# Layer 1 of a two-layer trunk step: both score maps of a query tile in one step, cached keys in a step of their own

## The chip, the core and the metric

The kernel is one launch on one NeuronCore of a Trainium2 chip. The metric is the device time of the launch in microseconds, median of several runs; less is better. The core has TensorE (PE: matmuls and transposes, with weight loads as a second stream, PEld), VectorE (DVE), ScalarE (ACT), GpSimd (POOL) and SyncE (SP, which here only starts weight loads). Each engine runs its own queue in order; semaphores tie the queues together. Matmul results land in PSUM, eight banks of 128 partitions x 512 fp32.

## What is computed

A two-layer trunk over 512 latent tokens and 128 context tokens, 2048 wide. Layer 0 is a gated MLP beside grouped-query attention. Layer 1, which the change touches, is differential attention with 16 heads: each head has two maps with 64-wide queries and keys, and one 128-wide value.

```python
def diff_attend(q, k, v, lam):
    scale = C_QK_DIM ** -0.5

    def block(qb):
        s = jnp.einsum('bqhmd,bshmd->bhmqs', qb, k).astype(F32) * scale
        p = jax.nn.softmax(s, axis=-1)
        w = (p[:, :, 0] - lam * p[:, :, 1]).astype(v.dtype)
        return jnp.einsum('bhqs,bshe->bqhe', w, v)
...
out = (o.reshape(b_, t, C_V_WIDTH) * jax.nn.silu(g)) @ w_out
```

Latent tokens read the 512 latent keys and 128 cached context keys in one softmax, so a query tile of 128 latent tokens has 640 keys; the context tile has 128 keys.

## The kernel before

**Projection.** Weights stream in as chunks of 512 columns: 16 slices of 128 rows (kt) for each chunk, 5 token tiles for each slice. fp32 is split in two parts, `hi` and `lo`, and each product is three matmuls (hi·hi, hi·lo, lo·hi). ACT casts a slice to `w_hi` (L676), DVE subtracts to get `w_lo` (L1032), both two slices ahead of PE, in a ring of four. A slot is one token tile of one slice: three matmuls of 512 columns (L495). A chunk has 80 slots.

**Attention beside it.** The attention of layer 1 is cut in steps, listed in `ORDER1`, and the list `AT1` says behind which slot each step is issued. Heads 0 to 11 take 60 slots each, in three groups (a loop of three chunks and four heads); heads 12 to 15 take 80 slots each, with the numbers of `AT1` times 6/5 (a loop of one chunk and one head). All three engines walk the same list: PE puts a step behind its slot; ACT and DVE put it behind the split of the slice in which the slot lies (slots 5k to 5k+4), in order. So within one slice ACT does one split and then the steps due, and so does DVE.

**The steps.** T0 to T2 turn q and k (transposes into PSUM bank 5, `TURN`; ACT casts the hi part, L626; DVE subtracts the lo part, L907, which frees the bank). S is one map of one query tile: 64 rows of the array, two halves of 320 keys into banks 6 and 7, three matmuls each (L382); then DVE takes the row maximum (L914) and scales it (L917), and ACT takes the exponential with its row sum (L637, with a read of the accumulator behind it). Eight S are wide (four query tiles, two maps), two are 128 keys wide (context tile). Behind both maps of tile u DVE combines them into one weight tile (`combine(u)`: L926, L928, L931). T3 to T9 turn the weights (T3 to T5 tiles 0 and 1, T6 to T8 tiles 2 and 3, T9 the context tile; PE L373). P multiplies with v (L391), B turns the result back (L398).

**Who waits for whom.** All turns, products and back turns share bank 5. PE starts T4 only when DVE has finished the subtract of T3 (`t_free`). PE starts T3 when `combine(1)` is done (`w_ready`), T6 when `combine(3)` is. On ACT the step T3 begins with the casts of v (L652, L653), on DVE with the subtracts of v (L968, L970), which wait for those casts. PE starts a score step when ACT has read the score before it (`s_exp`). `norm_out` of the head before is spread over DVE's steps. GpSimd loads the next head's q, k and v and rotates q and k (L1351 to L1358).

The two lists before:

```python
ORDER1 = ["T", "T", "T", "S", "S", "S", "S", "T", "S", "T", "S", "T", "S", "P", "S", "B", "S", "T", "S",
          "T", "T", "P", "B", "T", "P", "B"]
AT1 = [0, 2, 4, 7, 10, 14, 18, 24, 26, 28, 31, 32, 35, 36, 40, 41, 44, 45, 48, 49, 51, 52, 54, 56, 58, 59]
```

## Time and profile before

| | |
|---|---|
| median of 3 runs | 2920.69 us (2916.67 to 2921.15) |
| profiled execution, first to last instruction | 2917.0 us |
| granted TensorE clock, mean | 0.970 of 2.4 GHz |
| TensorE busy | 2717.5 us (93%) |
| VectorE busy | 1565.7 us (54%) |
| ScalarE busy | 1017.8 us (35%) |
| layer 1's groups of heads 0 to 11 | about 1503 to 2278 us |
| layer 1's heads 12 to 15 | to about 2576 us, 76.8 us each |

Starts and durations are in microseconds from the first instruction. Matmuls are pipelined and their ends are modelled, so the distance between starts says what TensorE spends; a wait shown in brackets can understate what was lost. Each attention step can be priced by taking two projection matmuls around it and subtracting the usual distance.

### The profile page before, as it was taken

Reading aid. Unit: us, or ns where it says so; the run is one execution under the profiler, and the core shown is the slowest. Engines: PE = TensorE matmul, PEld = TensorE weight load, DVE = VectorE, ACT = ScalarE, POOL = GpSimd, SP = SyncE. Lnnn points to the kernel's source line nnn. Section 1 sums busy time; section 2 is a strip of 40 time slices with the busy share of each in tenths; the row PEclk is TensorE's granted clock in tenths of the full one; section 3 lists DMA queues with packets and bytes.
Section 4 is the critical chain, followed back from the end, with each engine's and each line's share of the span. In section 5 each row is a group of like instructions: output and inputs, shape, how many; then the busy total and the mean of one; then the engine's idle time right before and its main releaser. Section 6 shows DMA issues by size and latency. Waiting matters only on the chain.

```text
span 2917.0 us, 40231 instructions
## 1 busy us (share of the span) xinstructions
PE 2717.5 (93%) x12498; PEld 2106.4 (72%) x12498; DVE 1565.7 (54%) x3018; ACT 1017.8 (35%) x2023; POOL 417.3 (14%) x483
## 2 busy tenths in 40 slices
PE   6799999999999899979999999999999999979995
PEld 3488777777777677767877777777777777757774
DVE  5762455555656644446245556655655555555443
ACT  6632343442333334323233333333333333333331
POOL 0000121121122100000121112222211211010001
PEclk9899999999999999989999999999999999979998
DMA  8833444433445545543322222222222222365444
GB/s 322 334 115 112 148 147 141 136 114 129 154 162 171 201 172 181 181 152 119 108 97 82 89 84 78 91 89 88 76 98 75 94 95 88 102 207 191 159 140 176
DMA packets 164952, 400.77 MB, mean 137 GB/s; under 512 B 12936, under 2 KB 14608, under 8 KB 159568
## 3 DMA queue, kind: packets, MB, share of 16 engines
q1 hardware_dynamic: 131104, 249.14, 26.2%
...
## 4 chain that ended last, share of the span: by engine, by line
PE 74%; DVE 13%; issue 4%; DVEq 4%; ACT 3%; DMA 2%; SPq 0%; ACTq 0%; POOL 0%; POOLq 0%
PE ps L495 55%; PE ps L515 5%; PE ps L382 5%; PE ps L373 3%; DVE w_lo L1032 3%; PE ps L391 3%; DMA w_raw<-in_w_ada_dram 1%; DVE small L914 1%; ACT w_hi L676 1%; DVE work L931 1%; PE ps L474 1%; DVEq L1106 1%; DVE work L1126 1%; PE ps L525 1%; DVE small L835 1%
## 5 line engine op out<-in xcount | busy, mean ns | idle before, releaser
L495 PE MATMUL ps<-w_hi,hT_hi 128*128 128x512 f32 x2800 | 1155.9, 413 | 7.9 <-issue 7.9
L495 PE MATMUL ps<-w_hi,hT_lo 128*128 128x512 f32 x2800 | 1103.6, 394 | 0.0
L495 PE MATMUL ps<-w_lo,hT_hi 128*128 128x512 f32 x2800 | 1100.5, 393 | 0.0
L1032 DVE TENSOR_TENSOR w_lo<-w_raw,w_hi 128x512 fp32r<-128x512 f32 x944 | 641.4, 707 | 683.6 <-ACT w_hi L676 668.0
L676 ACT CAST w_hi<-w_raw 128x512 fp32r<-128x512 f32 x944 | 570.6, 620 | 503.3 <-PE ps L495 452.0
L495 PEld LDWEIGHTS ps<-w_hi,hT_hi 128*128 128x128 f32 x2800 | 531.6, 190 | 136.5 <-issue 42.7
L495 PEld LDWEIGHTS ps<-w_hi,hT_lo 128*128 128x128 f32 x2800 | 529.7, 189 | 117.8
L495 PEld LDWEIGHTS ps<-w_lo,hT_hi 128*128 128x128 f32 x2800 | 532.0, 190 | 89.5
L637 ACT ACTIVATE work<-ps,small 128x640 f32<-128x640 f32 (+1 forms) x192 | 139.1, 725 | 563.8 <-DVE small L917 563.7
L515 PE MATMUL ps<-w_hi,cst 128*128 128x512 f32 x384 | 193.9, 505 | 40.2 <-DVE w_lo L1032 30.4
L914 DVE TENSOR_REDUCE small<-ps 128x1 f32<-128x640 f32 (+1 forms) x200 | 143.7, 718 | 123.4 <-PE ps L382 116.2
L515 PEld LDWEIGHTS ps<-w_hi,cst 128*128 128x128 f32 x384 | 78.7, 205 | 139.5 <-DVE w_lo L1032 126.6
L515 PE MATMUL ps<-w_lo,cst 128*128 128x512 f32 x384 | 162.1, 422 | 0.0
L907 DVE TENSOR_TENSOR wT_lo<-ps,wT_hi 128x512 fp32r<-128x512 f32 (+2 forms) x168 | 93.6, 557 | 114.8 <-ACT wT_hi L626 113.2
L626 ACT CAST wT_hi<-ps 128x512 fp32r<-128x512 f32 (+2 forms) x168 | 80.5, 479 | 212.4 <-PE ps L373 211.8
L373 PE MATMUL ps<-consts,work 128*128 128x128 f32 x744 | 122.8, 282 | 28.7 <-DVE work L931 17.4
L373 PEld LDWEIGHTS ps<-consts,work 128*128 128x128 f32 x744 | 89.5, 142 | 80.8 <-DVE work L931 24.0
L382 PE MATMUL ps<-kT_hi,qT_hi 64*128 64x320 f32 (+1 forms) x360 | 123.6, 343 | 5.1 <-ACT work L637 4.9
L382 PEld LDWEIGHTS ps<-kT_hi,qT_hi 64*128 64x128 f32 (+1 forms) x360 | 66.3, 184 | 64.3 <-issue 47.6
L382 PE MATMUL ps<-kT_lo,qT_hi 64*128 64x320 f32 (+1 forms) x360 | 108.7, 302 | 0.0
L382 PE MATMUL ps<-kT_hi,qT_lo 64*128 64x320 f32 (+1 forms) x360 | 108.5, 301 | 0.0
L474 PE MATMUL ps<-consts,work 128*128 128x128 f32 x320 | 55.8, 314 | 53.4 <-DVEq L1106 34.9
...
## 6 DMA issues: line engine op xcount, KB each, us to landing
...
```

The costliest lines, as they stand in the source:

```text
L373: last = nc.tensor.transpose(ps[:, TURN, n * P:(n + 1) * P], src, ident)
L382: last = nc.tensor.matmul(ps[:, SC + b, 0:w], qT[x][r0:r0 + L.dk, q0:q0 + P], kT[y][r0:r0 + L.dk, k0:k0 + w], start=(i == 0), stop=(i == 2))
L391: last = nc.tensor.matmul(ps[:, TURN, 0:width], vv[x][:, vt, :], wT[y][:, k, 0:width], start=(k == 0 and i == 0), stop=(k == len(tiles) - ...
L474: last = nc.tensor.transpose(ps[:, TURN + t // TS, t % TS * P:(t % TS + 1) * P], slot(F, kt // 4)[:, t, kt % 4 * P:(kt % 4 + 1) * P], ident)
L495: last = nc.tensor.matmul(ps[:, t, :], x[:, kt, t * P:(t + 1) * P], w[:, kt % RING, :], start=(kt == 0 and i == 0), stop=(kt == KT - 1 and ...
L515: last = nc.tensor.matmul(ps[:, MOD, :], cst[:, kt * 4:kt * 4 + P], w[:, kt % RING, :], start=(kt == 0 and i == 0), stop=(kt == KT - 1 and ...
L626: last = nc.scalar.copy(dst, ps[:, TURN, c0:c1])
L637: nc.scalar.activation(dst if src.ndim == 2 else dst.rearrange("p (b w) -> p b w", b=2), src, ACT.Exp, bias=small[:, 20 + m:21 + m], scale ...
L676: nc.scalar.copy(w_hi[:, kt % RING, :], w_raw[:, i % RAW, kt % 2, :]).then_inc(w_hi_ready, 1)
L907: last_op = nc.vector.tensor_tensor(lo, ps[:, TURN, c0:c1], hi.bitcast(F32), ALU.subtract)
L914: nc.vector.tensor_reduce(small[:, 22 + m:23 + m], src, AX_X if src.ndim == 2 else mybir.AxisListType.XY, ALU.max)
L1032: nc.vector.tensor_tensor(w_lo[:, kt % RING, :], w_raw[:, i % RAW, kt % 2, :], w_hi[:, kt % RING, :].bitcast(F32), ALU.subtract).then_inc( ...
```

## The change

For layer 1 the step S becomes one step for both maps of a query tile over the 512 latent keys: map 0 on array rows 0 to 63 into bank 6, map 1 on rows 64 to 127 into bank 7, matmuls in pairs. A new step C computes, once for each head, the scores of all four query tiles against the 128 cached keys, both maps, in both banks; ACT copies them to SBUF (`ctx_scores`, in `ws_t`). X is the context tile, both maps. K is a step of DVE alone: the first takes the maxima of the cached-key scores, the others are `combine(0)` to `combine(4)`, which was inside the S steps before. ACT's exponentials for a tile are now four: two of 512 from PSUM, which release the banks (`s_exp`), and two of 128 from SBUF, which release `combine` (`s_full`). DVE takes both maxima in one instruction and adds the two row sums. `rope_a`, `gq` and `gk` share one buffer, GpSimd rotates in place, layer 1's gate bias lies in `ws_t` and is loaded some instructions later, and `norm_out` advances at every step.

```diff
-ORDER1 = ["T", "T", "T", "S", "S", "S", "S", "T", "S", "T", "S", "T", "S", "P", "S", "B", "S", "T", "S",
-          "T", "T", "P", "B", "T", "P", "B"]
+ORDER1 = ["T", "T", "T", "C", "K", "S", "K", "S", "K", "S", "T", "T", "T", "K", "S", "P", "B", "K", "X", "T", "T", "T",
+          "K", "P", "B", "T", "P", "B"]
...
-AT1 = [0, 2, 4, 7, 10, 14, 18, 24, 26, 28, 31, 32, 35, 36, 40, 41, 44, 45, 48, 49, 51, 52, 54, 56, 58, 59]
+AT1 = [0, 2, 4, 8, 11, 12, 19, 20, 27, 28, 30, 32, 34, 36, 37, 39, 42, 43, 44, 46, 47, 49,
+       50, 51, 53, 54, 57, 59]
...
-        gq = sb("gq", [P, P])
-        gk = sb("gk", [P, P])
+        scr = sb("scr", [P, 6 * P])
+        rope_a = scr[:, 0:4 * P]
+        gq = scr[:, 4 * P:5 * P]
+        gk = scr[:, 5 * P:6 * P]
...
-        gate_bias = rope_a[:, :]
         ws_t = sb("ws_t", [P, 1024])
+        gate_bias = [rope_a, ws_t[:, 0:NC]]
+        ctx_scores = ws_t
...
+        ctx_sums = small[:, 78:86]
+        ctx_max = small[:, 86:94].rearrange("p (m u) -> p m u", m=2)
...
+        def diff_pe(pe, h):
...
+            def both_maps(out, q0, k0, width):
+
+                for i, (x, y) in enumerate(((0, 0), (0, 1), (1, 0))):
+                    for m in range(2):
+                        r = slice(64 * m, 64 * m + 64)
+                        last = nc.tensor.matmul(ps[:, SC + m, out:out + width], qT[x][r, q0:q0 + P],
+                                                kT[y][r, k0:k0 + width], start=(i == 0), stop=(i == 2))
+                return last
+
...
+                elif kind == "C":
+                    pe.wait_ge(s.t_free, h * NF + 4)
+                    scores_free(0)
+                    for t in range(TS):
+                        last = both_maps(t * P, t * P, TS * P, P)
+                    last.then_inc(s.s_ready, 1)
+                elif kind == "S":
+                    scores_free(1 + u)
+                    both_maps(0, u * P, 0, NC).then_inc(s.s_ready, 1)
+                    u += 1
+                elif kind == "X":
+                    scores_free(5)
+                    both_maps(0, TS * P, NTOK, P).then_inc(s.s_ready, 1)
...
+        def diff_act(act, h):
...
+            def exponent(dst, src, n, total):
+                m, u = n % 2, n // 2
+                return nc.scalar.activation(dst, src, ACT.Exp, bias=small[:, 20 + 2 * (u % 2) + m:21 + 2 * (u % 2) + m],
+                                            scale=L1.scale, accum_out=total[:, n:n + 1])
...
+                elif kind == "C":
+                    act.wait_ge(s.s_ready, h * 6 + 1)
+                    nc.scalar.copy(ctx_scores[:, :], ps[:, SC:SC + 2, :].rearrange("p a b -> p (a b)")).then_inc(s.s_exp, 1)
+                elif kind in ("S", "X"):
+                    act.drain()
+                    act.wait_ge(s.w_ready, h * 5 + (u + 1))
+                    act.wait_ge(s.s_max, h * 5 + (u + 1))
+                    dst = weights[:, 0:2, 0:NC] if kind == "S" else weights[:, 0:2, 0:P]
+                    width = NC if kind == "S" else P
+                    for m in range(2):
+                        last = exponent(dst[:, m, :], ps[:, SC + m, 0:width], 2 * u + m, sums)
+                    last.then_inc(s.s_exp, 1)
+                    if kind == "S":
+                        for m in range(2):
+                            at = (m * TS + u) * P
+                            last = exponent(weights[:, m, NC:NTOK], ctx_scores[:, at:at + P], 2 * u + m, ctx_sums)
+                        last.then_inc(s.s_full, 1)
+                    u += 1
+                elif kind == "P":
...
+        def diff_dve(dve, h, before):
...
+            def context_max():
+
+                dve.drain()
+                dve.wait_ge(s.s_exp, h * 6 + 2)
+                nc.vector.tensor_reduce(small[:, 86:94], ctx_scores.rearrange("p (x k) -> p x k", k=P), AX_X, ALU.max)
+                dve.drain()
+                nc.vector.tensor_scalar(small[:, 86:94], small[:, 86:94], -L1.scale, None, ALU.mult)
+
+            def scores(u):
+
+                bias = small[:, 20 + 2 * (u % 2):22 + 2 * (u % 2)]
+                dve.drain()
+                dve.wait_ge(s.s_ready, h * 6 + (u + 2))
+                nc.vector.tensor_reduce(small[:, 24:26], ps[:, SC:SC + 2, 0:NC if u < TS else P], AX_X, ALU.max)
+                dve.drain()
+                if u < TS:
+                    nc.vector.scalar_tensor_tensor(bias, small[:, 24:26], -L1.scale, ctx_max[:, :, u],
+                                                   ALU.mult, ALU.min).then_inc(s.s_max, 1)
+                else:
+                    nc.vector.tensor_scalar(bias, small[:, 24:26], -L1.scale, None, ALU.mult).then_inc(s.s_max, 1)
+
+            def combine(u):
+
+                width = 640 if u < TS else P
+                dst = weights[:, 2 + u % 2, :] if u < TS else wts_p[:, :]
+                n = slice(2 * u, 2 * u + 2)
+                dve.drain()
+                if u < TS:
+                    dve.wait_ge(s.s_full, h * 4 + (u + 1))
+                    nc.vector.tensor_tensor(sums[:, n], sums[:, n], ctx_sums[:, n], ALU.add)
+                    dve.drain()
+                else:
+                    dve.wait_ge(s.s_exp, h * 6 + 7)
+                nc.vector.reciprocal(inv_sums[:, n], sums[:, n])
+                dve.drain()
+                nc.vector.scalar_tensor_tensor(small[:, 26:27], sums[:, 2 * u:2 * u + 1], small[:, 12:13],
+                                               inv_sums[:, 2 * u + 1:2 * u + 2], ALU.mult, ALU.mult)
+                dve.drain()
+                nc.vector.scalar_tensor_tensor(dst, weights[:, 1, 0:width], small[:, 26:27], weights[:, 0, 0:width],
+                                               ALU.mult, ALU.add).then_inc(s.w_ready, 1)
...
+                elif kind in ("S", "X"):
+                    scores(n)
+                    n += 1
+                elif kind == "K":
+                    if k == 0:
+                        context_max()
+                    else:
+                        combine(k - 1)
+                    k += 1
...
-                    nc.gpsimd.tensor_tensor(rope_a[:, :], flat, rope_c[:, :], ALU.mult)
                     z4 = flat.rearrange(halves, s=2, j=half)
                     b4 = rope_b[:, :].rearrange(halves, s=2, j=half)
                     s4 = rope_s[:, :].rearrange(halves, s=2, j=half)
                     for k in range(2):
                         nc.gpsimd.tensor_tensor(b4[:, :, k, :], z4[:, :, 1 - k, :], s4[:, :, k, :], ALU.mult)
                     pool.drain()
-                    nc.gpsimd.tensor_tensor(flat, rope_a[:, :], rope_b[:, :], ALU.add)
+                    nc.gpsimd.tensor_tensor(flat, flat, rope_c[:, :], ALU.mult)
+                    pool.drain()
+                    nc.gpsimd.tensor_tensor(flat, flat, rope_b[:, :], ALU.add)
...
-            wait(gb_free, 4)
-            load_bias(1, 0)
             wait(S[1].v_split, 16)
             load_y(1, 0)
             store_head(L1, 14)
             free_head(L1, 14)
             wait(S[1].t_ready, 160)
+            wait(gb_free, 4)
+            load_bias(1, 0)
```

The order in which the instructions stand changes on all three engines. Three places show it, all in a head of the groups, from the score step of the last tile ahead of the first weight transpose to that transpose.

ACT before: exponential (L637), split (L676), v casts, T3's cast, split, exponential, T4's cast (L626).

```order
L637 ACTIVATE work,ssq<-ps,small 128x640
...
L676 CAST w_hi<-w_raw 128x512
...
L652 CAST v_hi<-work 128x640
L653 CAST v_hi<-work 128x128
L626 CAST wT_hi<-ps 128x512
...
L676 CAST w_hi<-w_raw 128x512
...
L637 ACTIVATE work,ssq<-ps,small 128x640
L626 CAST wT_hi<-ps 128x512
```

ACT after: L769 is the exponential, L819 the split, L783 and L784 the v casts, L764 the casts of T3 and T4.

```order
L769 ACTIVATE work,ssq<-ps,small 128x512 x2
L769 ACTIVATE work,small<-ws_t,small 128x128 x2
...
L819 CAST w_hi<-w_raw 128x512
...
L783 CAST v_hi<-work 128x640
L784 CAST v_hi<-work 128x128
...
L764 CAST wT_hi<-ps 128x512
...
L764 CAST wT_hi<-ps 128x512
```

Before, the exponential ahead of the v casts is that of tile 1's second map; now it is tile 2's, four instructions, and its slot (28) lies two slots ahead of T3 (30).

DVE before: maximum, split, `combine(1)` (L926 to L931), v subtracts, T3's subtract.

```order
L914 TENSOR_REDUCE small<-ps 128x1
L917 TENSOR_SCALAR small<-small 128x1
...
L1032 TENSOR_TENSOR w_lo<-w_raw,w_hi 128x512
...
L926 RECIPROCAL ssq<-ssq 128x2
L928 SCALAR_TENSOR_TENSOR small<-ssq,small 128x1
L931 SCALAR_TENSOR_TENSOR work<-work,small 128x640
...
L968 TENSOR_TENSOR v_lo<-work,v_hi 128x640
L970 TENSOR_TENSOR v_lo<-work,v_hi 128x128
L907 TENSOR_TENSOR wT_lo<-ps,wT_hi 128x512
```

DVE after: `combine(1)` (L1083 to L1092), tile 2's maximum (L1067, L1070), split (L1275), v subtracts, T3's subtract (L1051).

```order
L1083 TENSOR_TENSOR ssq<-ssq,small 128x2
L1087 RECIPROCAL ssq<-ssq 128x2
L1089 SCALAR_TENSOR_TENSOR small<-ssq,small 128x1
L1092 SCALAR_TENSOR_TENSOR work<-work,small 128x640
...
L1067 TENSOR_REDUCE small<-ps 128x2
L1070 SCALAR_TENSOR_TENSOR small<-small 128x2
...
L1275 TENSOR_TENSOR w_lo<-w_raw,w_hi 128x512
...
L1120 TENSOR_TENSOR v_lo<-work,v_hi 128x640
L1122 TENSOR_TENSOR v_lo<-work,v_hi 128x128
...
L1051 TENSOR_TENSOR wT_lo<-ps,wT_hi 128x512
```

A whole maximum of tile 2 now stands between `combine(1)` and the subtract that frees the bank for T4.

PE before, from a wide S (slot 26) to the T behind it (28): six matmuls, all on one half of the rows.

```order
L382 MATMUL ps<-kT_hi,qT_hi 128x320
L382 MATMUL ps<-kT_lo,qT_hi 128x320
L382 MATMUL ps<-kT_hi,qT_lo 128x320
L382 MATMUL ps<-kT_hi,qT_hi 128x320
L382 MATMUL ps<-kT_lo,qT_hi 128x320
L382 MATMUL ps<-kT_hi,qT_lo 128x320
...
L373 MATMUL ps<-consts,work 128x128 x4
```

PE after, from S of tile 2 (slot 28) over T3 (30) to T4 (32); L580 is the projection.

```order
L488 MATMUL ps<-kT_hi,qT_hi 128x512 x2
L488 MATMUL ps<-kT_lo,qT_hi 128x512 x2
L488 MATMUL ps<-kT_hi,qT_lo 128x512 x2
L580 MATMUL ps<-w_hi,hT_hi 128x512
...
L480 MATMUL ps<-consts,work 128x128 x4
...
L480 MATMUL ps<-consts,work 128x128 x4
```

There were four slots between T3 and T4; there are two.

## Rows read from the trace of the kernel before

**Rows 1.** The page: busy time, share of the span and instructions of each engine.
```profile
PE 2717.5 (93%) x12498; PEld 2106.4 (72%) x12498; DVE 1565.7 (54%) x3018; ACT 1017.8 (35%) x2023; POOL 417.3 (14%) x483
```

**Rows 2.** Windows: stretch, length; PE, PEld, DVE, ACT, POOL busy (count); clock, DMA, GB/s.
```profile
1780.00:2040.00 260.00, 248.09 (x1207) 190.71 (x1205) 151.53 (x319) 90.40 (x206) 55.95 (x59) 0.99 0.26 85
```

**Rows 3.** Timeline, a wide score step: start, duration, engine, line, tiles, forms.
```profile
2393.60 0.39 PE L495 MATMUL ps<-w_lo,hT_hi 128*128 128x512 f32 x1
...
2393.83 0.39 PE L495 MATMUL ps<-w_hi,hT_lo 128*128 128x512 f32 x1
...
2394.83 0.30 PE L382 MATMUL ps<-kT_lo,qT_hi 64*128 64x320 f32 x1
...
2394.98 0.31 PE L382 MATMUL ps<-kT_hi,qT_lo 64*128 64x320 f32 x1
...
2395.56 0.40 PE L495 MATMUL ps<-w_lo,hT_hi 128*128 128x512 f32 x1
```

**Rows 4.** Timeline, 1800 to 1803: a narrow score step, then a weight transpose.
```profile
1800.70 0.39 PE L495 MATMUL ps<-w_hi,hT_lo 128*128 128x512 f32 x1
...
1801.84 0.40 PE L495 MATMUL ps<-w_lo,hT_hi 128*128 128x512 f32 x1
...
1802.31 0.60 PE L373 MATMUL ps<-consts,work 128*128 128x128 f32 x4
...
1802.98 0.39 PE L495 MATMUL ps<-w_lo,hT_hi 128*128 128x512 f32 x1
```

**Rows 5.** Waits of TensorE, 1503 to 2576: total, times, longest.
```profile
PE ps L373 <- DVE work L931: 17.4, 13, 2.1
...
PE ps L382 <- ACT work L637: 4.9, 8, 1.3
PE ps L391 <- DVE wT_lo L907: 3.6, 16, 0.2
```

**Rows 6.** Groups by form, 1520 to 2278: busy, mean ns of one, idle before.
```profile
L914 DVE TENSOR_REDUCE small<-ps 128x1 f32<-128x640 f32 x91 | 75.1, 825 | 35.7 <-PE ps L382 30.8 <-issue 1.8
...
L914 DVE TENSOR_REDUCE small<-ps 128x1 f32<-128x128 f32 x24 | 7.0, 292 | 13.2 <-PE ps L382 12.9
...
L637 ACT ACTIVATE work<-ps,small 128x640 f32<-128x640 f32 x91 | 72.5, 796 | 269.4 <-DVE small L917 269.4
...
L637 ACT ACTIVATE work<-ps,small 128x128 f32<-128x128 f32 x24 | 8.8, 368 | 54.8 <-DVE small L917 54.8
```

**Rows 7.** Timeline of one head: exponential, split, v, combination, first weight transpose.
```profile
1832.21 0.79 ACT L637 ACTIVATE work<-ps,small 128x640 f32<-128x640 f32 x1 [5.23 <-DVE small L917]
...
1833.00 0.61 ACT L676 CAST w_hi<-w_raw 128x512 fp32r<-128x512 f32 x1
...
1837.65 0.72 ACT L652 CAST v_hi<-work 128x640 fp32r<-128x640 f32 x1
...
1838.28 0.29 ACT L653 CAST v_hi<-work 128x128 fp32r<-128x128 f32 x1
1838.64 0.17 DVE L926 RECIPROCAL ssq<-ssq 128x2 f32<-128x2 f32 x1 [0.16 <-issue]
...
1839.97 0.82 DVE L968 TENSOR_TENSOR v_lo<-work,v_hi 128x640 fp32r<-128x640 f32 x1
1840.11 0.66 PE L373 MATMUL ps<-consts,work 128*128 128x128 f32 x4 [1.47 <-DVE work L931]
...
1841.42 0.69 DVE L907 TENSOR_TENSOR wT_lo<-ps,wT_hi 128x512 fp32r<-128x512 f32 x1 [0.43 <-ACT wT_hi L626]
```

**Rows 8.** Timeline: a combination that stands beside GpSimd's rotation.
```profile
1828.99 1.98 DVE L931 SCALAR_TENSOR_TENSOR work<-work,small 128x640 f32<-128x640 f32 x1
```

**Rows 9.** A window behind a loop boundary (columns as in Rows 2), and TensorE's timeline there.
```profile
1748.00:1750.00 2.00, 2.00 (x6) 1.61 (x7) 0.69 (x1) 0.62 (x1) 0.00 (x0) 0.50 0.90 364
...
1747.99 0.79 PE L495 MATMUL ps<-w_hi,hT_hi 128*128 128x512 f32 x1 [3.54 <-issue]
...
1751.47 0.40 PE L495 MATMUL ps<-w_hi,hT_hi 128*128 128x512 f32 x1
```

142 lines of the change are left out of this document (130 added, 12 removed).

## The prediction

> **What bounds the kernel now.** The page comes first: TensorE is busy 93% of the span, no other engine over 54% [rows 1]. Then the windows, because an average over stages hides the stage in question: in one group of four heads TensorE is busy 248 of 260 us, VectorE 152 and ScalarE 90 [rows 2]. So layer 1's attention is bound by TensorE, and what TensorE spends on it counts in full. But the other two engines have slack only on average. The timeline shows how a head really runs: one score, its maximum, its exponential, and the next thing TensorE wants often depends on the end of that chain. The table of waits says how much of that is visible already: 17.4 us for combined weights, 4.9 for an exponential, 3.6 for a subtract ahead of a product [rows 5]. Starts lie a little further apart than these idle times say, so I take 30 us in all for the waits that this schedule now has and that the new one replaces.
>
> **What the change saves on TensorE.** Two projection matmuls start 0.23 us apart. From the last one ahead of a wide score step to the second behind it are 1.73 us; less two distances of 0.23, a wide score step costs 1.27 us [rows 3]. Its six matmuls of 320 columns start 0.15 apart (0.87), so 0.40 is the step's fixed part. A narrow one costs 1.14 - 0.46 = 0.68 [rows 4]. A head has eight wide and two narrow: 11.5 us. After the change, if the two matmuls of a pair run at once, S costs 0.40 + 3 x 0.23 = 1.09, four of them 4.4. C has 12 pairs of 128 columns. Transposes of that width start 0.11 us apart (four take 0.60, one about 0.27) [rows 4], so C is 0.35 + 12 x 0.11 = 1.7 if the weight loads of a pair overlap too and 0.35 + 24 x 0.11 = 3.0 if they do not; I take 2.2, nearer to overlap, since the matmuls are assumed to. X lies between 0.7 and 1.0, I take 0.8. Sum 7.4, saved 4.1 us a head, **66 us for 16 heads** (bounds 50 and 79). If pairs do not overlap at all, S is 0.40 + 6 x 0.23 = 1.78, the sum 11.1, and only some 5 us are saved.
>
> No row of this trace has two row halves at work together. The Trainium skill (TensorEngine Tiling (Array Packing), Key Properties) says that different tiles can execute loads and matmuls in parallel, which is the first case; whoever leaves the page out is left with the two bounds, 66 and 5.
>
> **What the change adds: the wait between T3 and T4.** This is the term that decides, and it does not lie on TensorE. T4 needs the bank that T3 filled, and the bank is free when DVE has done T3's subtract. On ACT the four exponentials of tile 2 stand ahead of T3's cast, since S of tile 2 is now in slot 28 and T3 in slot 30. I follow the chain from the end of `combine(1)`, which TensorE needs for T3 as well:
> - DVE, maximum over 1024 elements: 0.825 us at 640 and 0.292 at 128 give 1.04 ns an element, so 1.22 us [rows 6]; with the drains around it and the small instruction, 1.6 until ACT starts.
> - ACT, two exponentials of 512: 0.796 at 640 and 0.368 at 128 [rows 6] give 0.69; with the accumulator read and the overlap of neighbours (1832.21 to 1833.00 is 0.79 for 640 wide [rows 7]) 0.68 each, the narrow ones 0.36 each. Together 2.1.
> - ACT, the split of the next slice, which starts 0.5 ahead of what follows it, then the casts of v, 0.63 + 0.29 [rows 7]. Together 1.4.
> - DVE, v subtracts: 0.82 with the next one starting a little early, the second taken as long as the cast of its size, 0.29; with a drain 1.1. T3's subtract 0.69 [rows 7], and 0.1 for signals.
>
> The sum is 7.0 us. In that time TensorE has T3 (0.45: 1802.98 - 1801.84 less three distances of 0.23 [rows 4]) and two slots (1.4). So if TensorE is at T3 when `combine(1)` ends, it stands for 5.2 us at T4.
>
> Is it there at that time? One tile's round from maximum to maximum is: 3.7 to the end of the exponentials as above, split on ACT 0.6, split on DVE 0.7, `combine` 1.6 (1838.64 to 1840.11 with its drain [rows 7]) and 0.24 for the added sum: 6.9 us. TensorE spends 8 x 0.69 + 1.09 = 6.6 on the way from S to S. The round is the longer one, so faster matmuls only lead to earlier waits. Undisturbed, from S of tile 0 to T4 the chain takes 1.0 + 2 x 6.9 + 7.0 = 21.8 us and TensorE's own work 17.5: **4.3 us of waiting**. But GpSimd rotates the next head's q and k in this stretch, and beside it a combination took 1.98 us instead of 0.9 [rows 8], and in one head of four an evacuation of five copies stands in ACT's queue. I add 2.2, so 6.5 in all, of which some 5 at T4 and the rest at T3 and at S of tile 2. Twelve heads: 78 us. In heads 12 to 15 the slots are a fifth further apart; from S of tile 2 TensorE has 5.0 us of its own, the chain 7.9: 2.9 each, 12 us. **Sum 90** (bounds 64 without the disturbances, 108 with them doubled).
>
> **The smaller terms.** T7 follows T6 by one slot. T6, its cast and its subtract take 0.60 + 0.59 + 0.69 and gaps, 2.0 us; TensorE has 0.45 + 0.69 of its own: 0.9 at least, and ACT may come late from X's exponentials; I take 1.5, **24 us** (14 to 37). T9 behind its back turn and the group boundaries: **7 us**. The clock: after a wait of 3.54 us at a loop boundary the granted clock was 0.50 in the next two microseconds, that is 1.2 instead of 2.4 GHz, and from 1747.99 to 1751.47 TensorE did six projection matmuls and one turn of four, 6 x 0.23 + 0.45 = 1.8 us at full clock, in 3.5 [rows 9]. So such a wait costs 1.6 us more, for twelve heads **19 us** (0 if the wait at T4 stays shorter than that one). DVE's work for C, the rotation in place (same instruction count, one drain more) and the later gate bias (one issue, behind the last turn of head 15) hide beside the projection; if the bias comes late it costs under a microsecond, once.
>
> **The sum.** 90 + 24 + 7 + 19 = 140 us more, 66 + 30 = 96 us less: +44 on the profiled execution of 2917.0, which gives 2961. The runs' median lies 3.7 above that span: **2965 us**.
>
> The Trainium skill (TensorEngine Tiling (Array Packing), PSUM Bottleneck) warns that row tiling speeds up TensorE and not the evacuation of PSUM, which may then be the bound. That is this sum's direction; the page gives no figure for it, and nothing above is taken from it.
>
> **Rivals.**
> 1. *The pairs do not overlap.* Then 5 instead of 66 are saved (+61). Each S is 0.7 longer, so TensorE arrives about 2 us later at T4 in the groups and 0.7 in the last heads, which takes back 27. Result 2999. For it: all matmuls of the trace run one behind the other. Against: they all share rows or banks with their neighbours.
> 2. *Not slower: the ACT and DVE chain ahead of T4 is shorter than its parts.* Place: the subtract of T3. The gain of 96 stands against 24 + 7, and against 19 only if the clock falls; without that it pays as long as the heads wait less than 65 / 16 = 4.1 us each, where I have 5.6. The undisturbed 4.3 and 2.9 are close to that point. If the chain halves this to 2 to 2.5 a head with a full clock, 90 + 19 become 36: 2892. For it: the margin is small, and two of the three instructions I price by their size have no row of their own. Against: the queue order is fixed, and six instructions stand in it.
> 3. *Gain and waits cancel*: chain undisturbed, short T7, clock kept: 64 + 17 + 7 - 96 = -8, about 2915.
> 4. *Worse than the sum*: the clock stays at its lower level through more of each head, since T7, T3 and S wait as well; doubled clock term and upper bounds, 3030.
>
> **How the numbers follow.** Forecast 0.54, pairs serial 0.17, faster chain 0.14, cancel 0.08, worse 0.07. The forecast's own range is 2925 to 3005: all lower bounds but that of the clock at one end, all upper ones at the other. To hold 8 in 10 the range takes in the serial case and the upper part of "worse", and below the cancelling one: 2908 to 3025. A measurement of this kernel tells about 0.2% (6 us) from no change. Faster: the faster chain and half of the cancelling case, 0.18. Within 0.2%: part of the other half and the forecast's lowest end, 0.06. Slower: 0.76.
>
> **What would show it.** Pairs: the two matmuls of a pair start within some 10 ns and a wide step costs 1.1 us, not 1.8. The chain: in the table of waits a new line of some 60 us, TensorE's transpose waiting for DVE's `wT_lo`, longest about 5 us, 12 to 16 large ones, and ACT's v cast right behind four exponentials. The clock: windows behind T4 at 0.5. VectorE busy share must stay near 54%. The forecast is wrong if the transposes wait under 2 us at T4, or if groups of heads take less than 260 us; it is right for a wrong reason if the extra time lies outside 1503 to 2576.

## The result: slower by 3.9%, more than forecast

| kernel | median, us (lowest to highest) | ratio to the kernel before (95%) |
|---|---|---|
| before | 2920.92 (2916.67 to 2924.34) | 1 |
| changed | 3033.51 (3029.88 to 3037.02) | 1.0385 (1.0368 to 1.0401) |

The forecast was 2965, range 2908 to 3025. The direction was right and the main mechanism was there. The loss, +113 us, is more than twice the +44 of the sum, and the time lies 8 us above the range.

From the page of the changed kernel, the line of busy shares and the first line of its chain. TensorE is at 89% instead of 93% [rows 1], with the same number of instructions; the chain that ended last goes through TensorE for only 61% of the span.

```profile
PE 2706.4 (89%) x12498; PEld 2088.7 (69%) x12498; DVE 1595.2 (53%) x2954; ACT 1060.7 (35%) x2295; POOL 416.0 (14%) x483
...
PE 61%; DVE 19%; ACT 6%; DVEq 5%; issue 5%; DMA 2%; ACTq 2%; SPq 0%; POOL 0%; POOLq 0%
```

Everything ahead of 1503 us takes as long as before. Layer 1's stretch of projection and attention took 1503 to 2576 before and takes 1503 to 2692 now: 116 us, the whole difference. The window over it (columns as in [rows 2]) shows TensorE busy 1024 of 1189 us, at a granted clock of 0.93:

```profile
1503.00:2692.00 1189.00, 1024.13 (x5021) 780.87 (x5020) 651.11 (x1247) 415.62 (x1113) 209.44 (x222) 0.93 0.25 79
```

**The pairs work.** TensorE's timeline at a wide score step. `x2` means that both maps' matmuls are in the row. They start together, and the third pair starts 0.23 us after the second. Priced like the step of [rows 3], from the projection matmul at 1939.59 to the second one behind the step less two distances of 0.23, the step costs 1.09 us, as forecast.

```profile
1939.59 0.39 PE L580 MATMUL ps<-w_hi,hT_lo 128*128 128x512 f32 x1
1939.91 0.50 PE L488 MATMUL ps<-kT_hi,qT_hi 64*128 64x512 f32 x2
1940.24 0.39 PE L488 MATMUL ps<-kT_lo,qT_hi 64*128 64x512 f32 x2
1940.47 0.39 PE L488 MATMUL ps<-kT_hi,qT_lo 64*128 64x512 f32 x2
1940.80 0.50 PE L580 MATMUL ps<-w_hi,hT_hi 128*128 128x512 f32 x1
```

C costs 1.68 us and X 0.69, so the scores of a head fall from 11.5 to 6.73 us. Over 16 heads TensorE saves 77 us.

**The waits.** TensorE's waits from 1500 us on (total, times, longest), against those of [rows 5]. L480 is a transpose step, L488 a score step, L769 the exponential, L1051 the subtract of a turn.

```profile
PE ps L480 <- DVE wT_lo L1051: 102.5, 32, 5.5
PE ps L488 <- ACT work L769: 37.3, 13, 4.5
PE ps L480 <- DVE work L1092: 7.9, 11, 1.3
```

The first line stands for two waits a head, 32 in all: T4's, up to 5.5 us, and T7's, 1.5 to 2.

**The chain of T4, one head.** Rows of all engines from the end of `combine(1)` to T4 (L1092 combination, L1067 maximum, L819 the split of the next weight slice, L783 and L784 the casts of v, L764 the cast of T3):

```profile
1887.49 0.88 DVE L1092 SCALAR_TENSOR_TENSOR work<-work,small 128x640 f32<-128x640 f32 x1
1888.43 0.66 PE L480 MATMUL ps<-consts,work 128*128 128x128 f32 x4 [0.76 <-DVE work L1092]
1888.54 1.23 DVE L1067 TENSOR_REDUCE small<-ps 128x2 f32<-128x1024 f32 x1 [0.16 <-issue]
...
1890.38 0.69 ACT L769 ACTIVATE work<-ps,small 128x512 f32<-128x512 f32 x1 [4.55 <-DVE small L1070]
...
1892.49 0.61 ACT L819 CAST w_hi<-w_raw 128x512 fp32r<-128x512 f32 x1
1893.00 0.73 ACT L783 CAST v_hi<-work 128x640 fp32r<-128x640 f32 x1
...
1893.83 0.58 ACT L764 CAST wT_hi<-ps 128x512 fp32r<-128x512 f32 x1
1893.96 0.82 DVE L1120 TENSOR_TENSOR v_lo<-work,v_hi 128x640 fp32r<-128x640 f32 x1
...
1895.18 0.69 DVE L1051 TENSOR_TENSOR wT_lo<-ps,wT_hi 128x512 fp32r<-128x512 f32 x1 [0.20 <-issue]
...
1895.93 1.12 PE L480 MATMUL ps<-consts,work 128*128 128x128 f32 x4 [5.45 <-DVE wT_lo L1051]
```

From T3 to T4 are 7.50 us, where the prediction had 7.0 from the end of `combine(1)`. Between them stand the instructions that it named, in its order. The maximum is 1.23 for 1.22 expected, an exponential 0.69 for 0.69.

**The clock behind it.** A window that begins with this T4 has a granted clock of 0.56, and the matmuls of the projection in it stand 0.43 us apart instead of 0.23:

```profile
1896.00:1902.00 6.00, 6.00 (x19) 4.90 (x20) 1.96 (x4) 1.48 (x3) 2.07 (x3) 0.56 0.36 122
```

```profile
1897.27 0.63 PE L580 MATMUL ps<-w_lo,hT_hi 128*128 128x512 f32 x1
1897.70 0.63 PE L580 MATMUL ps<-w_hi,hT_lo 128*128 128x512 f32 x1
```

### The profile page after: what moved, and what is told of

It is laid out like the page before. It is cut to its first block, busy times and chain, and to the rows that moved or that the text cites. A ratio compares the mean times of both kernels' runs of the same rounds, so it can differ in the third digit from the quotient of the medians.

```text
span 3032.0 us, 40647 instructions
## 1 busy us (share of the span) xinstructions
PE 2706.4 (89%) x12498; PEld 2088.7 (69%) x12498; DVE 1595.2 (53%) x2954; ACT 1060.7 (35%) x2295; POOL 416.0 (14%) x483
## 4 chain that ended last, share of the span: by engine, by line
PE 61%; DVE 19%; ACT 6%; DVEq 5%; issue 5%; DMA 2%; ACTq 2%; SPq 0%; POOL 0%; POOLq 0%
PE ps L580 46%; PE ps L600 5%; DVE w_lo L1275 3%; ACT work L769 3%; DVE small L1067 3%; PE ps L480 2%; ACT w_hi L819 2%; DVE work L1092 2%; PE ps L535 2%; DMA w_raw<-in_w_ada_dram 1%; ACTq L791 1%; PE ps L559 1%; DVEq L1080 1%; PE ps L488 1%; PE ps L379 1%
## 5 line engine op out<-in xcount | busy, mean ns | idle before, releaser
L580 PE MATMUL ps<-w_hi,hT_hi 128*128 128x512 f32 x2800 | 1171.1, 418 | 13.6 <-issue 7.3
L580 PE MATMUL ps<-w_hi,hT_lo 128*128 128x512 f32 x2800 | 1118.7, 400 | 0.0
L580 PE MATMUL ps<-w_lo,hT_hi 128*128 128x512 f32 x2800 | 1116.7, 399 | 0.0
L1275 DVE TENSOR_TENSOR w_lo<-w_raw,w_hi 128x512 fp32r<-128x512 f32 x944 | 648.2, 714 | 786.4 <-ACT w_hi L819 770.8
L819 ACT CAST w_hi<-w_raw 128x512 fp32r<-128x512 f32 x944 | 569.1, 620 | 502.8 <-PE ps L580 452.2
L580 PEld LDWEIGHTS ps<-w_hi,hT_hi 128*128 128x128 f32 x2800 | 543.3, 194 | 149.2 <-issue 41.3
L580 PEld LDWEIGHTS ps<-w_hi,hT_lo 128*128 128x128 f32 x2800 | 540.2, 193 | 121.5
L580 PEld LDWEIGHTS ps<-w_lo,hT_hi 128*128 128x128 f32 x2800 | 543.5, 194 | 94.0
L769 ACT ACTIVATE work<-ps,small 128x512 f32<-128x512 f32 (+1 forms) x160 | 98.3, 619 | 407.2 <-DVE small L1070 336.4
L480 PE MATMUL ps<-consts,work 128*128 128x128 f32 x496 | 96.2, 317 | 114.5 <-DVE wT_lo L1051 102.5
L480 PEld LDWEIGHTS ps<-consts,work 128*128 128x128 f32 x496 | 65.1, 160 | 164.9 <-DVE wT_lo L1051 122.9
L1051 DVE TENSOR_TENSOR wT_lo<-ps,wT_hi 128x512 fp32r<-128x512 f32 (+2 forms) x112 | 62.4, 557 | 111.3 <-ACT wT_hi L764 108.2
L1598 POOL TENSOR_TENSOR work<-work,rope_s 128x256 f32<-128x256 f32 x96 | 80.0, 851 | 247.7 <-DVEq L1014 162.3
L764 ACT CAST wT_hi<-ps 128x512 fp32r<-128x512 f32 (+2 forms) x112 | 53.7, 479 | 160.6 <-PE ps L480 160.6
L559 PE MATMUL ps<-consts,work 128*128 128x128 f32 x320 | 55.6, 313 | 51.5 <-DVEq L1349 32.9
L1067 DVE TENSOR_REDUCE small<-ps 128x2 f32<-128x1024 f32 (+1 forms) x80 | 85.2, 1065 | 15.9 <-issue 9.1
L1570 POOL DMA_DIRECT2D work<-z x48 | 41.6, 869 | 376.3 <-PE ps L480 279.4
L488 PE MATMUL ps<-kT_hi,qT_hi 64*128 64x128 f32 (+1 forms) x288 | 57.0, 392 | 37.3 <-ACT work L769 37.3
```

Source lines behind the costliest of these rows:

```text
L480: last = nc.tensor.transpose(ps[:, TURN, n * P:(n + 1) * P], src, ident)
L488: last = nc.tensor.matmul(ps[:, SC + m, out:out + width], qT[x][r, q0:q0 + P], kT[y][r, k0:k0 + width], start=(i == 0), stop=(i == 2))
L559: last = nc.tensor.transpose(ps[:, TURN + t // TS, t % TS * P:(t % TS + 1) * P], slot(F, kt // 4)[:, t, kt % 4 * P:(kt % 4 + 1) * P], ident)
L580: last = nc.tensor.matmul(ps[:, t, :], x[:, kt, t * P:(t + 1) * P], w[:, kt % RING, :], start=(kt == 0 and i == 0), stop=(kt == KT - 1 and ...
L769: return nc.scalar.activation(dst, src, ACT.Exp, bias=small[:, 20 + 2 * (u % 2) + m:21 + 2 * (u % 2) + m], scale=L1.scale, accum_out=total ...
L819: nc.scalar.copy(w_hi[:, kt % RING, :], w_raw[:, i % RAW, kt % 2, :]).then_inc(w_hi_ready, 1)
```

## Where the 116 us went

The timeline gives the start of each step and of each projection matmul in the stretch. From the distance over a step I take what the step costs undisturbed.

| what | forecast | found in starts |
|---|---|---|
| T4 over its own 0.45 us, 16 heads | } | 91 |
| S steps over 1.09 us | } 90 | 45 |
| T3 over 0.45 us | } | 12 |
| T7 | } 31, with T9 and the group boundaries | 29 |
| chunk ends and loop boundaries | } | about 6 |
| projection matmuls 0.40 us or more apart (half clock) | 19 | 42 |
| score steps themselves | -66 | -77 |
| waits of the schedule before | -30 | -30 (as forecast, not counted anew) |
| sum | +44 | +118, against 116 |

In the stretch 186 distances between projection matmuls lie between 0.40 and 0.65 us and cost 43.6 us over 0.23; before there were 8, 2.0 us. That is the clock's line of the table.

The two ends agree better than the lines do. Counted by starts, the kernel before waited 20 us at T3, 6 at its score steps and 8 at its second product, 34 and not 30. About 7 us of slow distances right behind a step stand in the step's line and in the clock's as well. And T5 and T8, each the last part of a group of turns, have no line: they cost 12 us over their undisturbed time now and 3 before.

The block of waits was forecast with 90 and is 148: T4 alone takes what was meant for all three. Most of the rest stands in front of S. The rows of DVE and GpSimd behind a maximum show why. L1602 and L1600 are GpSimd's rotation of the next head's q and k; L980, L1083 and L1089 work on 1 to 5 columns; L1033 is a piece of the normalisation of the head before:

```profile
1943.87 1.28 POOL L1602 TENSOR_TENSOR work<-work 128x512 f32<-128x512 f32 x1
1944.08 1.10 DVE L980 SCALAR_TENSOR_TENSOR small<-small 128x5 f32<-128x5 f32 x1
...
1947.46 1.56 POOL L1600 TENSOR_TENSOR work<-work,rope_c 128x512 f32<-128x512 f32 x1
1948.04 1.00 DVE L1083 TENSOR_TENSOR ssq<-ssq,small 128x2 f32<-128x2 f32 x1 [0.17 <-issue]
...
1949.16 1.28 POOL L1602 TENSOR_TENSOR work<-work 128x512 f32<-128x512 f32 x1
1949.36 1.10 DVE L1089 SCALAR_TENSOR_TENSOR small<-ssq,small 128x1 f32<-128x1 f32 x1
...
1951.52 0.82 DVE L1033 TENSOR_TENSOR work<-work,gsub 128x640 f32<-128x640 f32 x1
```

Away from the rotation L980 takes 0.17, L1083 0.16 and L1089 0.22 (at 1941.79, 1886.72 and 1887.20). Here each ends within 0.03 us of the GpSimd instruction beside it: 1945.18 and 1945.15, 1949.04 and 1949.02, 1950.46 and 1950.44. They are held until GpSimd is through. The Trainium skill (SBUF — State Buffer, Who interferes with whom) gives that rule: a VectorE instruction with two inputs in SBUF contends with a GpSimd instruction that reads SBUF, and the ports that they share are an exclusive lock. The trace agrees by these three ends, and by the instructions with at most one SBUF input, whose means do not move with the rotation (below).

So the first round, from the maximum of tile 0 to that of tile 1, is here 11.1 us (1942.27 to 1953.39), not 6.9. S of tile 2, at 1956.45, waited 3.36 us for the exponentials at the end of that round. It is so in every head of the groups that was measured (heads 1 to 11): the first round takes 11.1 to 11.4 us and the second 7.0. In the head above neither the rotation nor a piece of the normalisation stands in the second.

## Experiments

The theory: TensorE waits at S and T4 for a chain of VectorE and ScalarE, and the order of steps and their slots put that chain there, not the pairs. Rivals: the slots alone are at fault; the pairs are worth nothing; the half clock is the loss; the rotation or the normalisation costs every kernel the same. The kernel before, timed anew beside each group of experiments, took 2917.7 to 2919.3 us.

### The order and the slots

**S2 behind the turns.** S of tile 2 is put behind T5, and the slots are set so that TensorE finds each step ready.

```
-ORDER1 = [T, T, T, C, K, S, K, S, K, S, T, T, T, K, S, P, B, K, X, T, T, T, K, P, B, T, P, B]
-AT1 = [0, 2, 4, 8, 11, 12, 19, 20, 27, 28, 30, 32, 34, 36, 37, 39, 42, 43, 44, 46, 47, 49, 50, 51, 53, 54, 57, 59]
+ORDER1 = [T, T, T, C, K, S, K, S, K, T, T, T, S, K, P, S, B, K, T, X, T, T, K, P, B, T, P, B]
+AT1 = [0, 2, 4, 7, 8, 10, 10, 21, 21, 33, 36, 38, 38, 38, 41, 41, 44, 44, 51, 51, 53, 55, 55, 56, 57, 58, 59, 59]
```

> The changed kernel with its step functions untouched and only the two lists altered: the score step of tile 2 stands behind T5 instead of ahead of T3, and the slots leave room (T3 33, T4 36, T5 38, S of tiles 2 and 3 in 38 and 41, X 51). Theory (the order in ScalarE's and VectorE's queues makes the waits, the steps themselves are sound): T4 no longer stands behind four exponentials, its wait falls from about 5.7 us a head to under 1, the waits of the wide scores from 45 us in all to under 10, and the 77 us that the paired matmuls save on TensorE become visible: 2850 us, 2830 to 2890, and so faster than the kernel before. Rival (the paired form as such is too dear for the other two engines: more exponentials, wider maxima): the waits only move to other steps, 2990 to 3050.

Measured 2874.17 us (2867.20 to 2879.92), ratio 0.9853 (0.9832 to 0.9873): 159 us less than the changed kernel and faster than the kernel before, with the same arithmetic. It came out 24 us above the 2850 expected, within its range, and the waits (L478 is the transpose, L578 the projection here) say where the rest is: not at T4 any more, but at the projection, for a split.

```profile
PE ps L578 <- DVE w_lo L1273: 19.9, 14, 3.0
PE ps L478 <- DVE wT_lo L1049: 8.7, 24, 0.5
```

**The order alone.** The same table, with S of tile 2 back ahead of T3.

```
-ORDER1 = [T, T, T, C, K, S, K, S, K, T, T, T, S, K, P, S, ...]
-AT1 = [0, 2, 4, 7, 8, 10, 10, 21, 21, 33, 36, 38, 38, 38, 41, 41, ...]
+ORDER1 = [T, T, T, C, K, S, K, S, K, S, T, T, T, K, P, S, ...]
+AT1 = [0, 2, 4, 7, 8, 10, 10, 21, 21, 30, 33, 36, 38, 38, 41, 41, ...]
```

> The version with S2 behind the turns (2874.2 us), with its slots, but S2 put back ahead of T3 (slot 30) as in the changed kernel. It tells the order from the slots. Theory: S2's maxima and exponentials stand on VectorE and ScalarE ahead of the combination, copies and splits that T4 waits for, some 3 us on each; with 3 slots between T3 and T4, T4 waits again: 2950 (2925 to 2975). Rival, only the slots matter: 2885 or less.

Measured 2945.61 us (2940.45 to 2950.01), ratio 1.0090 (1.0062 to 1.0117), as expected. The wait of the turns is back, and only that one; the waits of S for an exponential are 0.9 us in all:

```profile
PE ps L478 <- DVE wT_lo L1049: 59.3, 28, 4.6
```

So one step moved past three, with its slot, is worth 71 us (2945.6 against 2874.2), 4.5 a head. Of these 51 stand in the turns' wait (59.3 against 8.7) and 20 in distances at half clock (24.5 against 4.9). The maximum, exponentials and combination of a tile whose scores no one needs yet stood ahead of work that T4 needed.

**Room alone.** The changed kernel's order, with four more slots between T3 and T4.

```
-AT1 = [..., 27, 28, 30, 32, 34, 36, 37, 39, ...]
+AT1 = [..., 27, 28, 30, 36, 38, 38, 38, 39, ...]
```

> The changed kernel with its order of steps, and only the slots of T4 (32 to 36), T5 (34 to 38), K3 and S3 (to 38) changed: four more slots of projection, some 2.8 us, lie between T3 and T4. Theory, the wait of T4 is the time from T3 through combination, copies, splits and rounding less what TensorE has to do meanwhile: the wait falls from 5.5 to about 2.7 us, 45 us over 16 heads, of which a part comes back in front of S3, P0 and T7, and the half clock behind it goes, up to 20 us: 2980 (2965 to 3000). Rival, a round of engines without end of which T4 is only one place: the time lost moves to other steps and the total stays within 10 us of 3033.

Measured 3004.12 us (3001.43 to 3004.98), ratio 1.0297 (1.0280 to 1.0315): 29 us less, where 54 were expected. The transposes' waits fell by 37 us as the theory has it, to at most 2.7 us. But 16.5 us of waits for the first product's copy (L806) came up, as P and B keep their old slots, and S still waits. The rival, that the total stays within 10 us of 3033, is out too:

```profile
PE ps L478 <- DVE wT_lo L1049: 65.6, 32, 2.7
PE ps L486 <- ACT work L767: 34.7, 12, 4.1
PE ps L540 <- ACT oT L806: 16.5, 16, 1.8
```

The four tables make a ladder: 3033.5 as it is, 3004.1 with room at T4, 2945.6 with the table of "S2 behind the turns" but S of tile 2 ahead of T3, 2874.2 with S of tile 2 moved as well. The last step, S of tile 2 alone, is worth 71 us. The 88 us ahead of it come from the slots, and from two changes of order that go with them: the first P stands ahead of S of tile 3, and T6 ahead of X. No run parts these from the slots. So the rival "only the slots" is out, and the place of S of tile 2 isn't the whole either.

### What stretches the chain

**No rotation.** Layer 1's rotary embedding is left out, GpSimd's work of that stretch.

```
-                for z in (q_in, k_in):
+                for z in (q_in, k_in) if L.n == 0 else ():
```

> The changed kernel without the rotary rotation of q and k in layer 1 (GpSimd's four instructions per tensor are left out there; layer 0 keeps it). Theory: the extra 45 us of waits at the wide scores come from VectorE's small instructions that take 1.0 to 1.3 us beside GpSimd's rotation instead of 0.2; without it these waits fall to about 10 us, T4's wait stays at 5 us a head: 2985 us, 2965 to 3005. Rival (the waits at the scores come from the round's own length and from the instructions of norm_out): under 15 us are gained, 3018 or more.

Measured 2985.78 us (2985.29 to 2986.35), ratio 1.0228 (1.0209 to 1.0246): 48 us less than the changed kernel, as expected. The wait at T4 did not move:

```profile
PE ps L480 <- DVE wT_lo L1051: 104.7, 32, 5.5
```

L488's wait for an exponential is 4.8 us in all here, where it was 37.3. The distances at half clock fell as well, from 43.6 to 31.5 us. The first round takes 8.8 us instead of some 11.2, and the second 7.0 as before. By form, from 1503 to 2576 us, the small instruction L1083 has a mean of 161 ns here and 347 in the changed kernel, L980 165 and 280, the split L1275 691 and 770. The maximum L1067, which reads PSUM, has 1224 and 1225, and the turn's subtract L1051, with one input in PSUM, 689 and 690.

**The same in the kernel before.**

```
-                for z in (q_in, k_in):
+                for z in (q_in, k_in) if L.n == 0 else ():
```

> The kernel before with layer 1's rotary embedding left out (its GpSimd work; the output is another). On the changed kernel this gave 48 us. Theory: there VectorE's short instructions, stretched beside GpSimd, stand in a chain that TensorE waits for; before they do not, so little changes: 2914 (2908 to 2919) against 2918. Rival, the rotation costs every kernel the same through VectorE: 2870 to 2890.

Measured 2905.2 us (2899.92 to 2907.89), ratio 0.9956 (0.9942 to 0.9969): 13 us, somewhat more than the 4 expected, a quarter of the 48. VectorE's instructions were stretched before as well (the split of weights had a mean of 715 ns, and 688 without rotation), but TensorE hardly stood behind them: its wait for combined weights fell from 17.4 to 9.8 us and that for an exponential from 4.9 to nothing. The price of a disturbance depends on who waits.

**Normalisation off K and X.** The pieces of the normalisation of the head before are no longer advanced at the steps K and X, so they don't stand between a maximum and the combination.

```
-                next(before, None)
+                if kind not in ("K", "X"):
+                    next(before, None)
```

> The changed kernel with norm_out of the head before not advancing at the steps K and X, so that none of its pieces stands between the maxima of the cached keys and the maximum of tile 0, nor between combine(0) and the maximum of tile 1 (0.8 us each). They run behind the scores instead, beside ScalarE's exponentials. Theory: the round of tiles 0 to 2 gets 1 to 1.6 us shorter in the twelve heads of the groups: 3017 us, 3008 to 3025. Rival (those pieces are hidden, the round is held by ScalarE and the rotation): 3033, within 5.

Measured 3004.59 us (3002.64 to 3009.77), ratio 1.0296 (1.0274 to 1.0318): 29 us less, where 16 were expected. The first round takes 9.7 to 9.8 us in heads 1 to 10. S's wait falls to 11.4 us and the distances at half clock to 29.9, while T3's wait grows:

```profile
PE ps L480 <- DVE wT_lo L1051: 108.3, 32, 5.5
PE ps L480 <- DVE work L1092: 19.1, 18, 1.3
PE ps L488 <- ACT work L769: 11.4, 9, 2.6
```

**Both: S2 behind the turns, normalisation off K and X.** The two edits above, together.

> The version with S2 behind the turns, with the normalisation of the head before not advanced at the steps K and X. Theory: on the changed kernel this was worth 29 us because VectorE's chain set the length; here it does not, so little is left: 2868 (2860 to 2876) against 2874.2. Rival, VectorE's order still sets it: 2850 or less.

Measured 2847.01 us (2846.34 to 2849.68), ratio 0.9761 (0.9745 to 0.9777). This is the fastest: 71 us under the kernel before, 186 under the changed one. My expectation was wrong, and its rival right: VectorE's order still cost 27 us. I had looked at T4 and S, where little was left to gain. DVE's rows of the kernel without this edit show what was missed: a piece of the normalisation (L1031) beside the rotation takes 1.73 us instead of 0.82, the two splits behind it come late, and the projection waits 1.03 us for them.

```profile
1876.37 1.73 DVE L1031 TENSOR_TENSOR work<-work,gsub 128x640 f32<-128x640 f32 x1
1878.29 2.10 DVE L1273 TENSOR_TENSOR w_lo<-w_raw,w_hi 128x512 fp32r<-128x512 f32 x2 [0.19 <-issue]
...
1879.84 0.50 PE L578 MATMUL ps<-w_hi,hT_hi 128*128 128x512 f32 x1 [1.03 <-DVE w_lo L1273]
```

With the edit the projection's wait for splits in the stretch is 1.4 us in all, down from 19.9, which is 18.5 of the 27, and TensorE is busy 970 of its 1001 us:

```profile
1503.00:2504.00 1001.00, 969.60 (x5013) 743.25 (x5012) 637.60 (x1242) 416.13 (x1109) 208.20 (x222) 0.99 0.29 93
```

### What the pairs are worth

**Maps in turn (loops exchanged).**

```
-                for i, (x, y) in enumerate(((0, 0), (0, 1), (1, 0))):
-                    for m in range(2):
+                for m in range(2):
+                    for i, (x, y) in enumerate(((0, 0), (0, 1), (1, 0))):
```

> The changed kernel with only the pairing undone: in each score step the three matmuls of map 0 come first, then the three of map 1, so neighbours share the same half of the rows. Theory (VectorE and ScalarE's chain is the bound in each head): a wide step costs 1.8 instead of 1.09 us and C 3.0 instead of 1.68, together some 4.4 us a head or 71 us in all, but 60% of it is taken back by shorter waits at T4, T3 and the scores: 3062 us, 3050 to 3080. Rival (TensorE's own time still counts in full): 3033 + 71 = 3104.

Measured 3034.16 us (3029.05 to 3037.60), ratio 1.0398 (1.0378 to 1.0418), 0.7 us from the changed kernel: neither the 3062 of the theory nor the rival's 3104. The order of TensorE's instructions did change. In the built program map 0's three matmuls now stand ahead of map 1's three. The timeline still shows pairs:

```profile
1935.34 0.51 PE L488 MATMUL ps<-kT_hi,qT_hi 64*128 64x512 f32 x2
1935.67 0.40 PE L488 MATMUL ps<-kT_lo,qT_hi 64*128 64x512 f32 x2
```

A trace of the new order, and not a repeat of the old one, can be told by a small thing: read one by one, the two matmuls of a pair start 10 ns apart (median of 63 wide steps), and 3 ns in the changed kernel. So the edit did not undo the overlap, and its time says nothing of what the overlap is worth.

**Maps apart.** The same order, with a wait between the two triples that is always satisfied.

```
+                for m in range(2):
+                    if m == 1:
+                        pe.wait_ge(setup_in, 16 * N_SETUP)
+                    for i, (x, y) in enumerate(((0, 0), (0, 1), (1, 0))):
```

> The changed kernel, but the three matmuls of map 0 stand ahead of the three of map 1 in every scores step, with a wait that is always satisfied between them, so that the two halves of the rows no longer work on neighbouring matmuls (but for one at the joint). All other engines get the same work in the same order. Theory, the maxima, exponentials and splits from one step to T4 set the length of a head: the matmuls that are no longer paired lengthen TensorE's work by some 0.45 us a scores step and about 3 us a head, 45 us in all (from 0.23 us for a matmul of 512 columns), and part of that goes into waits that get shorter: 3055 (3045 to 3070) against 3033.5. Rival, TensorE's own work sets the length: all of it counts, 3079 or more. Rival, pairing was worth nothing: 3033.

> The version with S2 behind the turns (2874.2 us), with the maps apart in the same way. Here TensorE waits little, so the same 3 us a head should count in full: 2919 (2905 to 2935), which would say that the two halves of the rows are worth about 45 us once nothing else holds the engine. If other engines set the length here too, less than 20 us.

Measured 3033.30 us (3030.52 to 3038.03) and, for the version with S2 behind the turns, 2875.70 (2871.94 to 2885.36; ratio 0.9861): the times of 3033.5 and 2874.2 again, so the rival "pairing was worth nothing" seems right. The timeline says otherwise. Although map 0's three matmuls come ahead of map 1's, the trace has them side by side again, and the step still takes 1.09:

```profile
1881.86 0.50 PE L490 MATMUL ps<-kT_hi,qT_hi 64*128 64x512 f32 x2
1882.19 0.40 PE L490 MATMUL ps<-kT_lo,qT_hi 64*128 64x512 f32 x2
1882.42 0.41 PE L490 MATMUL ps<-kT_hi,qT_lo 64*128 64x512 f32 x2
```

The two halves of the rows had three matmuls each and worked them off at the same time. Map 1's first weight load, which carries the wait and stands in the program behind map 0's three matmuls, starts at 1881.86, 10 ns after map 0's first load and 0.33 us ahead of map 0's second matmul. Over the wide steps of both kernels the two matmuls of a pair start 10 ns apart in the median. The expectation was wrong in its premise, that only neighbours can overlap. The edit had not undone the cause.

**Map 1 waits for map 0.** A real dependency, on the fastest version.

```
+                for m in range(2):
+                    if m == 1:
+                        half[0] += 1
+                        last.then_inc(s.half, 1)
+                        pe.wait_ge(s.half, h * 9 + half[0])
```

> The version with S2 behind the turns and the normalisation off K and X (2847.0 us), but in every scores step the three matmuls of map 1 wait for the end of map 0's three, so that the two halves of the rows cannot work at once. Written order alone did not part them: with map 0's matmuls written ahead, the trace still shows both maps' rows at the same starts. Theory: side by side they save TensorE 0.23 us a matmul of 512 columns, and here TensorE sets the length: a wide step goes from 1.09 to 1.8 to 2.0 us (three more matmuls and the end of the third to wait for), C from 1.7 to some 3.8, X by 0.5, about 6 us a head and 96 us in all: 2943 (2915 to 2960), that is, no faster than the kernel before. Rival, other engines set the length and absorb it: below 2885.

Measured 2939.16 us (2935.38 to 2945.92), ratio 1.0081 (1.0054 to 1.0109), as expected, 92 us more than with pairs. Now the rows are single, and the second triple starts 0.45 us after the start of the first triple's last matmul:

```profile
1893.15 0.49 PE L493 MATMUL ps<-kT_hi,qT_hi 64*128 64x512 f32 x1
1893.49 0.39 PE L493 MATMUL ps<-kT_lo,qT_hi 64*128 64x512 f32 x1
1893.72 0.39 PE L493 MATMUL ps<-kT_hi,qT_lo 64*128 64x512 f32 x1
1894.17 0.50 PE L493 MATMUL ps<-kT_hi,qT_hi 64*128 64x512 f32 x1
```

In C the end of one quarter's map 1 and the start of the next quarter's map 0 have no wait between them, and there the triples run side by side again, out of the order in which they are written:

```profile
1886.65 0.27 PE L493 MATMUL ps<-kT_hi,qT_lo 64*128 64x128 f32 x1
1886.98 0.33 PE L493 MATMUL ps<-kT_hi,qT_hi 64*128 64x128 f32 x2
```

A wide step costs 2.10 instead of 1.09, C 3.17 instead of 1.68, X 0.61 more: 6.1 us a head, 98 over 16, of which 92 arrive in the time. Some 0.32 of each wide step's 1.01 is the wait for the end, which a kernel without pairs wouldn't have; without it 0.69, three matmuls of 0.23. The distances at half clock grew too, from 2.6 to 11.1 us, mostly behind C. So the 92 us are more than the pairs alone are worth. An estimate for those: 0.69 for each wide step, 12 x 0.11 for C and 3 x 0.11 for X are 4.4 us a head, 70 us in all. On a schedule that leaves TensorE the bound, lost time on TensorE counts nearly in full, so the pairs pay. Whether they pay on the changed kernel too, where TensorE waits, wasn't run.

### The clock

**The wait filled.** The changed kernel, with 14 more matmuls a head ahead of T4; their result is not used.

```
+                        if r == 4:
+                            scores_free(4)
+                            for _ in range(14):
+                                nc.tensor.matmul(ps[:, SC, 0:NC], qT[0][:, 0:P], kT[0][:, 0:NC], start=True, stop=True)
```

> The changed kernel with 14 matmuls more per head (512 columns, into the scores bank of map 0 once S2's exponentials have read it; S3 overwrites what they write), put ahead of T4, in the time that TensorE waits there: about 3.2 of the 5.5 us. Their result is not used, and nothing else changes. Theory, the half clock that follows each of these waits costs time of its own: after the wait at 1895.93 us a row of projections stands 0.43 us apart where it is 0.23 otherwise, 12 rows, 2.4 us a head, 38 us over 16 heads. With the wait filled the clock stays full and T4 starts as before, so the kernel gets faster although it does more: 2997 (2990 to 3010) against 3033.5. Rival, the half clock costs nothing of its own, as the engines behind it set the pace there too: 3030 to 3040. Rival, the matmuls delay T4: above 3040.

Measured 3018.41 us (3014.48 to 3020.70), ratio 1.0346 (1.0322 to 1.0369): 15 us less than the changed kernel, between the theory's 36 and the rival's nothing. The kernel does more and is faster, and the distances at half clock fell by 18 us, so the half clock has a price of its own. In the head from above T4 now waits 0.58 us and the projection behind it runs at full clock:

```profile
1883.18 3.47 PE L511 MATMUL ps<-kT_hi,qT_hi 128*128 128x512 f32 x14 [1.41 <-ACT work L773]
1887.23 0.66 PE L480 MATMUL ps<-consts,work 128*128 128x128 f32 x4 [0.58 <-DVE wT_lo L1055]
...
1904.94 0.66 PE L480 MATMUL ps<-consts,work 128*128 128x128 f32 x4 [1.99 <-DVE wT_lo L1055]
```

The last row is T7 of the same head. Its wait is 1.99 us, and the projection matmuls from 1905.66 to 1908.07 stand 0.43 apart, which they do not behind T7 in the changed kernel. Over the stretch, distances of 0.40 to 0.65 us fall from 186 (43.6 us) to 110 (25.7 us): behind T4 from 104 to none, behind T7 they rise from 21 to 51, and behind S of tiles 1 and 2 they stay near 50. The size was wrong for two reasons: I multiplied the head with 12 slow matmuls behind T4 by 16, although 186 over all waits are 12 a head in total, and a part of the slow stretches came back behind another wait.

## The prediction, point by point

- **TensorE bound before: right.** Without the rotation the kernel before gained only 13 us, and what that kernel lost at half clock is 2 us.
- **The saving, 66: right in kind, 11 short.** S was exact (1.09), C was taken as 2.2 and is 1.68, its lower bound; X 0.8 and is 0.69. Rival 1, pairs that don't overlap, is out.
- **The chain from T3 to T4: right.** 7.5 us for 7.0, the instructions that it named, 5.45 us of waiting for 5.2.
- **The block of waits, 90: the step that failed.** It was built as a balance of one head: the chain from S of tile 0 to T4, 21.8 us, plus 2.2 for disturbances, against 17.5 of TensorE's own work. The balance was sound, and the chain in it was too short. In heads 1 to 11 it takes 27.2 to 28.2 us. Two terms make the difference. To the first maximum the prediction had 1.0 us, and it is 1.9 to 2.4, as the maxima of the cached keys (1.22 us, L1058) and small instructions of the normalisation stand ahead of it on DVE. The first round was put at 6.9 and is 11.1 to 11.4. The second round (7.0 for 6.9) and what follows it were right. So TensorE pays 148 us at S, T3 and T4 instead of 90, of which T4 takes 91. The disturbances had been read from one instruction, the combination of 1.98 us [rows 8]; the small instructions that GpSimd holds up (0.16 to 0.22 becomes 1.0 or 1.1) and the normalisation's pieces in front of a maximum were left out. The experiments give these two 48 and 29 us (singly, on the changed kernel), and bring the first round to 8.8 and 9.8 us. The upper bound, 108, doubled too small a term, and by its own terms it should read 116 (12 x 8.7 + 12).
- **The last four heads: failed.** The block had 2.9 us each for them, since their slots are further apart. T4's excess was 4.6 to 6.3 in all 16 heads, and in three of the last four S added 1.3 to 1.6. Between T3 and T4 lie two slots there too.
- **T7, T9 and the boundaries, 31: right,** 35, of which T7 has 29.
- **The clock, 19: too small, 42.** It was counted once a head for twelve heads, from a loop boundary [rows 9], and slow distances follow waits at S and T7 too (47 and 21 of the 186). Rival 4 had named this, with a price that doubled it to 38.
- **VectorE's share near 54%: right,** 53%. **The extra time lies in 1503 to 2576 (now 2692): right.**
- **Rivals 2 and 3, faster or level:** out for this table. With another order and other slots the kernel is faster than the one before (2874, 2847), so "slower" was a result of the order and slots, as the prediction had it, and not of the pairs.
- **The range:** its ends, 2925 and 3005, don't come out of the bounds exactly. With the saving left at 66 they give 2929 and 2996.

Sum of the corrections: +58 in the block, +23 for the clock, -11 for the saving, +4 for T7, T9 and the boundaries: 44 + 74 = 118. The direction wasn't luck: the wait at T4, the wait at T7 and the saving came out near their size, and the first round, left too short, only adds to the loss.
